# A conformer, gated linear attention and banded attention kernel on one core: VectorE takes part of the lower halves, and the copies of the bias go out in four

## The reference

```python
def conformer_mixer(h, w_in, b_in, w_dw, b_dw, norm_g, norm_b, w_out, b_out):
    u = h @ w_in + b_in
    a, ga, z = jnp.split(u, 3, axis=-1)
    glu = a * jax.nn.sigmoid(ga)
    c = lax.conv_general_dilated(
...
    c = jax.nn.silu(layer_norm(c, norm_g, norm_b))
    return (c * jax.nn.silu(z)) @ w_out + b_out
...
        h = layer_norm(DN_ALPHA * h + y, post_ln_g[i], post_ln_b[i])
...
    bias = rel_bias.astype(jnp.float32)[t5_bucket(rel)]
```

## Time and profile before

| what | value |
|---|---|
| median of 3 runs | 2415.98 us (2415.59 to 2420.63) |
| the profiled execution, its own time | 2417.53 us |
| its span | 2415.8 us |
| PE busy | 2328.9 us, 96% |
| DVE, ACT, POOL busy | 1385.9, 1126.7, 876.8 us |

### The profile page before, as it was taken

How to read it: one execution, slowest core, us unless ns; L and a number is a source line. 1 busy time by engine, 2 the same in 40 slices (tenths; PEclk the granted TensorE clock), 3 DMA queues, 4 the chain that set the end, 5 groups by cost and what they waited for, 6 DMA issues and landing times. The chain is left out here.

```text
span 2415.8 us, 34621 instructions
## 1 busy us (share of the span) xinstructions
PE 2328.9 (96%) x13338; PEld 1215.4 (50%) x13338; DVE 1385.9 (57%) x2328; ACT 1126.7 (47%) x2181; POOL 876.8 (36%) x673
## 2 busy tenths in 40 slices
PE   8999999998997999999999998989899999999998
PEld 4555555543444455555555554444545554444443
DVE  6999999975554234334334334577467777235422
ACT  7766666576653234334334333233246666323311
POOL 3988888877883110100101101344023333000000
PEclk9999999998998999999999999999999999999999
DMA  5011111143333000100000002533100000101222
GB/s 204 27 55 40 39 45 35 49 137 100 115 125 138 28 1 5 53 1 32 18 1 14 1 1 94 100 121 115 62 23 15 19 1 2 40 18 64 103 105 88
DMA packets 52218, 134.67 MB, mean 56 GB/s; under 512 B 5391, under 2 KB 23439, under 8 KB 51032
## 3 DMA queue, kind: packets, MB, share of 16 engines
q1 hardware_dynamic: 52056, 132.46, 16.5%
HBM read 96.65 MB, written 35.80 MB: 55 GB/s over the span
## 5 line engine op out<-in xcount | busy, mean ns | idle before, releaser
L1155 DVE SCALAR_TENSOR_TENSOR cv_tap_sum<-cv_glu,cv_prm,cv_tap_sum 128x1024 f32<-128x1024 f32 x326 | 418.9, 1288 | 11.9 <-ACT cv_tap_sum L657 2.4
L911 POOL TENSOR_TENSOR mixed<-mixed,cv_tap_products 128x1024 f32<-128x1024 f32 x153 | 364.2, 2381 | 77.6 <-ACT cv_tap_products L672 62.1
L100 PE MATMUL cv_proj<-H_hi,cv_w_ga 128*128 128x416 f16 (+1 forms) x640 | 217.2, 339 | 8.1 <-DVE H_lo L1128 8.1
L101 PE MATMUL cv_proj<-H_lo,cv_w_ga 128*128 128x416 f16 (+1 forms) x640 | 217.2, 339 | 0.0
L102 PE MATMUL cv_proj<-H_hi,cv_w_ga 128*128 128x416 f16 (+1 forms) x640 | 217.1, 339 | 0.0
L100 PE MATMUL gm_vr<-gm_wvr_hi,H_hi 128*128 128x512 f16 (+1 forms) x544 | 202.8, 373 | 0.0
L101 PE MATMUL gm_vr<-gm_wvr_lo,H_hi 128*128 128x512 f16 (+1 forms) x544 | 202.8, 373 | 0.0
L102 PE MATMUL gm_vr<-gm_wvr_hi,H_lo 128*128 128x512 f16 (+1 forms) x544 | 202.8, 373 | 0.0
L1823 POOL TENSOR_TENSOR gm_q_inter<-gm_q_rel,gm_block_decays 128x512 f32<-128x512 f32 x16 | 16.8, 1049 | 467.1 <-ACT gm_block_decays L1900 467.1
L672 ACT ACTIVATE cv_tap_products<-cv_glu,cv_prm 128x1024 f32<-128x1024 f32 x138 | 151.8, 1140 | 35.8 <-POOL mixed L911 35.7
L2179 DVE SCALAR_TENSOR_TENSOR gm_v_r<-gm_vr,gm_v_r 128x256 f32<-128x256 f32 x64 | 27.2, 425 | 236.8 <-ACT gm_v_r L1919 236.8
(11 more groups left out here) (449 smaller groups left out, 5783.3 us busy)
## 6 DMA issues: line engine op xcount, KB each, us to landing
cv_w_stage<-conv_w SPq DMA_DIRECT2D x24, 512.0 KB, 4.0
mixed<-gla_w SPq DMA_DIRECT2D x8, 1024.0 KB, 6.9
go_rows<-h_rows SPq DMA_DIRECT2D x16, 512.0 KB, 4.1
h_rows<-go_rows SPq DMA_DIRECT2D x16, 512.0 KB, 2.9
pl_sums_a<-h_rows SPq DMA_DIRECT2D x16, 512.0 KB, 3.5
out<-pl_sums_a SPq DMA_DIRECT2D x16, 512.0 KB, 2.6
cv_tap_products<-gate_z SPq DMA_DIRECT2D x24, 256.0 KB, 3.9
mixed<-xT SPq DMA_DIRECT2D x12, 416.0 KB, 8.7
```

The source lines that it names most:

```text
L100: nc.tensor.matmul(out, w_hi, x_hi, start=first, stop=False)
L101: nc.tensor.matmul(out, w_hi, x_lo, start=False, stop=False)
L911: nc.gpsimd.tensor_tensor(c_unit(U), c_unit(U), prod[:, r % 3, :], ALU.add).then_inc(s_add, 1)
L1155: nc.vector.scalar_tensor_tensor(out=acc_unit(U), in0=window(U, k), scalar=col(U // 2, k), in1=acc_unit(U), op0=ALU.mult, op1=ALU.add).the ...
```

## The change

In the convolution's rows, ACT copies the sums of group 2 in the middle of gating group 1, and those of groups 3 and 4 before it scales the row of that step and not after it. VectorE makes 11 of the lower halves in place of POOL: `LOWS_AT` gives the step, the group and the tiles. The bias of the output is fetched and scaled ahead of the first gating of group 1, and two more gates of that group are loaded ahead of the norm's vectors. The last row is transposed into banks of its own, its scaling comes in two halves, and DVE does the lower half of row 14 ahead of the last row's g and b. In the output layer the bias table is written in four pieces of two heads, in steps 4 to 7 behind the load of the row, where it was one piece in step 2. The k weights are split at the end of step 14 and not at the start of step 15.

```diff
+        LOWS_AT = {3: (2, (5,)), 4: (2, (6, 7)), 7: (3, (4, 5)), 8: (3, (6, 7)), 11: (4, (4, 5)), 12: (4, (6, 7))}
+        DVE_LOWS = [T * KT + k for T, ks in LOWS_AT.values() for k in ks]
...
         pt = [acc[:, HALF + 512 * h:HALF + 512 * h + 512] for h in range(2)]
+        last_pt = [acc[:, 512 * h:512 * h + 512] for h in range(2)]
...
+        def turned(s, h):
...
+        def wait_low(eng, n):
+            by_dve = sum(x < n for x in DVE_LOWS)
+            if by_dve:
+                eng.wait_ge(c_lod, by_dve)
+            eng.wait_ge(c_lo, n - by_dve)
...
@@ -581,18 +596,18 @@
                 load_row(0)
                 for b in range(2):
                     sp.wait_ge(s_szo[b], 16 * KT * NTT // 2)
-                sp.wait_ge(s_add, slot(UNITS - 1, n_products(UNITS - 1)) + 1)
-                for k in range(R):
-                    load_gate(1, k)
                 sp.wait_ge(o_lo, KT)
                 vector(bias_bc, bias_dram, s_bv)
                 load_row(1)
+                sp.wait_ge(s_add, slot(UNITS - 1, n_products(UNITS - 1)) + 1)
+                for k in range(R + 2):
+                    load_gate(1, k)
                 sp.wait_ge(c_m, KT)
                 vector(g_bc, g_dram, s_vec)
                 vector(b_bc, b_dram, s_vec)
                 for s in range(NS + 1):
                     if s == 0:
-                        for k in range(R, KT):
+                        for k in range(R + 2, KT):
...
                 squares(2, range(CG))
-                gated(1, range(2))
                 act.wait_ge(s_bv, 16)
                 nc.scalar.activation(bias_bc, bias_bc, ACT.Copy, scale=1.0 / ALPHA).then_inc(s_bias, 1)
+                gated(1, range(2))
                 squares(2, range(CG, KT))
+                gated(1, range(2, 6))
+                copy_sums(2)
+                gated(1, range(6, KT))
                 for s in range(NS + 2):
-                    gated(*UNITS_AT.get(s, (0, ())))
-                    if (s, 0) in SUMS:
-                        copy_sums(SUMS[s, 0])
+                    if s:
+                        gated(*UNITS_AT.get(s, (0, ())))
...
+                                                 turned(s - 2, h).rearrange("p (k n) -> p k n", k=4)[:, :, 0:n],
+                                                 ACT.Copy).then_inc(s_th, 1)
+                    if (s, 1) in SUMS:
+                        copy_sums(SUMS[s, 1])
...
                         act.wait_ge(s_nm, s + 1)
-                        nc.scalar.activation(tile(s), tile(s), ACT.Identity, scale=sd[0:n, b, 1:2],
...
-                        copy_sums(SUMS[s, 1])
+                        for h in range(2) if s == LAST else (slice(0, 2),):
+                            x = tile(s).rearrange("p (a n) -> p a n", a=2)[:, h]
+                            mm = nc.scalar.activation(x, x, ACT.Identity, scale=sd[0:n, b, 1:2], bias=sd[0:n, b, 2:3])
...
                         gate(T, k)
-                        if i:
+                        if i and T * KT + ks[i - 1] not in DVE_LOWS:
                             low(T, ks[i - 1])
-                    if len(ks):
+                    if len(ks) and T * KT + ks[-1] not in DVE_LOWS:
                         low(T, ks[-1])
...
                                         pattern=[[-1, P]], channel_multiplier=1).then_inc(s_id, 1)
+                add_bias(0)
                 gated(1, range(2))
-                add_bias(0)
...
-                        if s:
+                        if s == LAST:
+                            pe.wait_ge(c_n, len(GROUPS) * KT)
+                        elif s:
...
-                            mm = nc.tensor.transpose(pt[h][:, q * P:q * P + n], tile(s)[:, c:c + P], ident[0:n, 0:n])
+                            mm = nc.tensor.transpose(turned(s, h)[:, q * P:q * P + n], tile(s)[:, c:c + P], ident[0:n, 0:n])
...
-                        pe.wait_ge(c_lo, (T + 1) * KT)
+                        wait_low(pe, (T + 1) * KT)
...
+                def gated_low(T, k):
+                    dve.wait_ge(c_hi, T * KT + k + 1)
+                    nc.vector.tensor_tensor(c_half(T, k, 1), silu_at(T, k), c_half(T, k, 0), ALU.subtract).then_inc(c_lod, 1)
...
-                    if s == LAST:
...
+                                                    turned(s - 2, h).rearrange("p (k n) -> p k n", k=4)[:, :, 0:n],
                                                     H_hi[:, 4 * h:4 * h + 4, at:at + n], ALU.subtract).then_inc(s_tl, 1)
+                    if s in LOWS_AT:
+                        T, ks = LOWS_AT[s]
+                        for k in ks:
+                            gated_low(T, k)
+                    if s == LAST:
+                        for h in range(2):
+                            c = slice(h * 512, h * 512 + 512)
+                            dve.wait_ge(s_vec, 16 * 2)
+                            dve.wait_ge(s_u, NS + h)
+                            nc.vector.tensor_tensor(tile(LAST)[:, c], tile(LAST)[:, c], g_bc[:, c], ALU.mult).then_inc(s_lg, 1)
+                            dve.wait_ge(s_lg, h + 1)
+                            nc.vector.tensor_tensor(tile(LAST)[:, c], tile(LAST)[:, c], b_bc[:, c], ALU.add).then_inc(s_lh, 1)
...
+        COPIES = range(4, 4 + HEADS // 2)
...
                 for s in range(NR):
-                    if s == 2:
-                        sp.wait_ge(s_bs, 1)
-                        rows = bass.AP(copies.tensor, copies.offset, [[(P + 1) * PITCH, HEADS], [PITCH, P + 1], [1, PITCH]])
-                        sp.dma_start(rows, spread_rows(vec, P + 1)).then_inc(s_bo, 16)
                     if s >= 2:
                         store_row(s - 2)
                     if 4 <= s + 1 < NR:
                         load_row(s + 1)
+                    if s in COPIES:
+                        heads = slice(2 * COPIES.index(s), 2 * COPIES.index(s) + 2)
+                        sp.wait_ge(s_bs, 1)
+                        rows = bass.AP(copies.tensor, copies.offset + heads.start * (P + 1) * PITCH,
+                                       [[(P + 1) * PITCH, 2], [PITCH, P + 1], [1, PITCH]])
+                        sp.dma_start(rows, spread_rows(vec[heads, :], P + 1)).then_inc(s_bo, 16)
...
-                    if s == END:
-                        act.wait_ge(ahead.sem, next_loaded)
-                        nc.scalar.activation(wkv[0][:, 0].rearrange("p k n -> p (k n)"), attn_slot(M, 0), ACT.Copy,
-                                             scale=WS).then_inc(s_kh, 1)
...
+                    if s == END - 1:
+                        act.wait_ge(ahead.sem, next_loaded)
+                        nc.scalar.activation(wkv[0][:, 0].rearrange("p k n -> p (k n)"), attn_slot(M, 0), ACT.Copy,
+                                             scale=WS).then_inc(s_kh, 1)
...
-                    if s == END:
-                        dve.wait_ge(s_bo, 16)
-                        dve.wait_ge(s_kh, 1)
...
+                    if s == END - 1:
+                        dve.wait_ge(s_bo, 16 * len(COPIES))
+                        dve.wait_ge(s_kh, 1)
```

More of the change, by code:

```diff
@@ L299, in conv_layer @@
         c_d, c_n, c_sl, c_m = m.sem("c_centred"), m.sem("c_normed"), m.sem("c_silu"), m.sem("c_gated")
-        c_hi, c_lo = m.sem("c_hi"), m.sem("c_lo")
+        c_hi, c_lo, c_lod = m.sem("c_hi"), m.sem("c_lo"), m.sem("c_lo_by_dve")
         c_sz = [m.sem(f"siluz_loaded{k}") for k in range(KT)]
@@ L450, in in_two @@
             return ap.rearrange("p (a n) -> p a n", a=2)
+        def turned(s, h):
+            return (last_pt if s == LAST else pt)[h]
         def n_of(s):
@@ L737, in silu @@
                         if k >= R0:
-                            act.wait_ge(c_lo, n - R0 + 1)
+                            wait_low(act, n - R0 + 1)
                     elif n >= KT + R:
-                        act.wait_ge(c_lo, n - R + 1)
+                        wait_low(act, n - R + 1)
                     else:
@@ L883, in _ @@
                             nc.scalar.activation(H_hi[:, 4 * h:4 * h + 4, at:at + n],
-                                                 pt[h].rearrange("p (k n) -> p k n", k=4)[:, :, 0:n], ACT.Copy).then_inc(s_th, 1)
+                                                 turned(s - 2, h).rearrange("p (k n) -> p k n", k=4)[:, :, 0:n],
+                                                 ACT.Copy).then_inc(s_th, 1)
+                    if (s, 1) in SUMS:
+                        copy_sums(SUMS[s, 1])
                     if s < NS:
@@ L889, in _ @@
                         act.wait_ge(s_nm, s + 1)
-                        nc.scalar.activation(tile(s), tile(s), ACT.Identity, scale=sd[0:n, b, 1:2],
-                                             bias=sd[0:n, b, 2:3]).then_inc(s_u, 1)
-                    if (s, 1) in SUMS:
-                        copy_sums(SUMS[s, 1])
+                        for h in range(2) if s == LAST else (slice(0, 2),):
+                            x = tile(s).rearrange("p (a n) -> p a n", a=2)[:, h]
```

(28 more changed lines are left out.)

## The result

The changed kernel takes **2450.97 us** (median of 4 runs, 2450.25 to 2452.25) where the kernel before took 2415.93 in runs on the same chip: a ratio of 1.0139, interval 1.0127 to 1.0151. It is slower. The forecast was 2448.6 with a range of 2412 to 2464. The profiled span grew from 2415.8 to 2449.7 us, by 33.9, against a forecast of 32.6.

The account below looks back on a forecast made before the run. PE works nearly all of the span, so only its waits can go or new ones come. Convolution +13.5, table pieces +23.5 and k weights -4.4 make +32.6 on 2415.98: 2448.6 us, range 2412 to 2464.

Parts of the forecast that it names:

- A: Convolution, sums of group 2: ACT's copies start sooner, the 7.03 us wait goes, all behind moves by -3.6 us.
- B: Convolution, row 5: waits for DVE's lower halves behind row 4's work, +3.8 us, with the restart +5.4.
- C: Convolution, row 9: waits for DVE's halves like row 5, +12.7 us, with the restart +14.3.
- D: Convolution, row 13: DVE's halves, slowed beside POOL, start it 8.5 us after row 12's end; convolution then at +17.2.
- E: Convolution's end: own banks and split scaling let the last transposes start sooner, -3.7 us; convolution in all +13.5.
- F: Output layer, bias table: each piece takes 21.5 us and delays row loads, +23.5 us at row 11; chance 0.60.
- G: Output layer's end: k weights split a row sooner, so last norms and transposes come 4.4 us sooner.
- Rival H: Output layer: pieces run at their engines' rate, 11 us each, so not slower: 2414.1 us; chance 0.17.
- J: Output layer: each head keeps its rate, 43 us a piece, row 11 another 86 later: about 2535 us; chance 0.10.
- K: Output layer: pieces of about 16 us or on different engines: 2426.7, up to 2436 us; chance 0.13 with L.
- L: Convolution: row 5 doesn't wait for DVE's halves, so it gains 7.3 us: 2427.8 us; counted in K's chance.

Follow-up runs that it names:

- both losses undone: The changed kernel with all lower halves on POOL and the table's pieces of heads four partitions apart: 2393.79 us, ratio 0.9903 to the kernel before.

## Why the prediction was right, point by point

The prediction gave 2448.6 us and a loss from two causes, VectorE's halves behind a row's own work and pieces read from neighbouring partitions. Both are what the experiments found. Shifts are between the traces of before and after; forecast in brackets.

- **A, right.** Row 2 began at 554.54 (554.95), released by POOL. The transposes behind group 2's chain moved from 584.87 to 580.75, by -4.1 (-3.6).
- **B, right.** Row 5 at 612.13 (612.6). Its products took 12.80 us (612.13 to 624.93), so the restart cost 2.4 and not 1.6. PE waited 12.31 and not some 9: it was done with row 4 9.2 us sooner than before (the transposes at 598.78 for 607.94) and not 3.6, since the sums of group 3 came sooner too, a gain that the forecast hadn't. It was lost at row 5, which starts by DVE's time; with all halves on POOL it counts.
- **C, right.** The totals of group 4 at 657.13 (657.3), row 9 at 673.13 (672.5). The wait of 12 us that the prediction's last part names is a slip: its own terms give about 7, and it was 8.08.
- **D, right.** DVE had row 12's second half at 720.05; row 13 began at 728.22, 8.4 after the row's end (8.5). That POOL holds DVE here was read from the earlier trace rows, and the 3.43 for 1.29 shows it.
- **E, right in size**, -4.2 (-3.7): PE's last full row ended 19.7 us later (755.03 before, 774.70 after), the next layer began 15.5 later. **Convolution +15.5 (13.5)**; the 2 us are the restarts, which the forecast priced by the one row of before with a short idle. The transposes behind the last full row (778.54) were still released by `H_lo`, and only those of the last row by DVE's b. The GLA layer gave 1.1 back, not forecast.
- **F, right in mechanism and size**: 21 us a piece (21.5). The estimate from the port figure of the Trainium skill, "SBUF — State Buffer", section "Door 1: The DMA port swizzle (why `[64,N]` ≈ `[32,N]`)", gave 19.1; the rate was 25 GB/s here and not 27.6. Row 9's load was used at 1663.23; the forecast, moved by the 14.4 of the layers ahead, says 1665.6. Row 11 at 1674.69 (1677.1). F cost +21.4 up to the transposes at 1731.93 (23.5). My reason, that two heads share something, is shown by the heads four apart: 25 to 51 GB/s on two engines. The halfway value itself was a choice between the far bounds of 11 and 43, and that it came out so near was luck; it did since two neighbours now share what four shared before. What it lacked: I took the old stall to come of the store queued behind the write alone. On ACT's queue it stayed, with a slow load in the store's place.
- **G, right**: -4.0 at the transposes that it names (1708.67 before, 1740.56 after, row 15 having ended 35.9 later; forecast -4.4). Up to the last transposes it is -5.6, and -5.2 alone: the 1.6 more are TensorE's clock, which before was at a mean of 0.66 from 1708 to 1712 and now was 1.00 in the same place.
- **Not forecast, +3.6** behind the output layer: attention and its last stretch took 3.0 us longer (the last stretch at a lower clock, below), 0.4 lie in the change of layers, and 0.2 behind them.

Sum: 15.5 - 1.1 + 21.4 - 5.6 + 3.6 = 33.8, of the span's 33.9. The terms missed by +2.0, -1.1, -2.1, -1.2 and +3.6; that this leaves 1.2 is luck, too.

Rival H (pieces at their engines' rate) is what happens with heads four apart: 2420.38, where H said 2414.1. Of the 6.3 between them, 1.4 lie in the convolution (the next layer at 786.49, 14.9 later than before), 2.9 in attention (321.1 us for 318.2), and 1.7 in the kernel before itself, which took 2417.64 in those runs. J (each head keeps its rate) is refuted by the window of 25 GB/s for two heads where eight had 49. K (pieces of 16 us, or on different engines): a piece took 21, and in the window from 1604 to 1612 two engines were busy though a further piece had been issued at 1599.38, so pieces didn't run side by side. L is refuted by the waits of B to D.

## What to carry to other kernels

Before work is moved to an engine with idle time, look at what stands ahead of it there in the same step: an engine that is 57% busy can still be the last one that a row waits for, if the helper's work stands behind the row's own. Time it beside what the other engine does then, too: two halves took 1.29 us by themselves and 3.43 beside POOL's scaling. When a transfer from few partitions is slow, look at which partitions it reads before it is cut into pieces; a cut changes how often others wait for it, a stride changes how long it lasts. Where a change has many parts, an experiment that undoes each shows a version that keeps the good ones: here 57 us lay between it and the whole.

## What the runs showed of the hardware

**Neighbouring partitions.** A write from partitions 0 to 7 ran at 49 GB/s on eight engines, two heads side by side at 25 on two, two heads four apart at 51 on two, eight heads four apart at 224 on eight. The 25 for two and the 49 for eight fit groups of four partitions that share 25; distances other than one and four were not run. The Trainium skill, "SBUF — State Buffer", section "Door 1: The DMA port swizzle (why `[64,N]` ≈ `[32,N]`)", has partitions 0 to 3 on one port and gives 27.6 GB/s measured for it; the 25, and the 49 for two ports, agree within 12%.

**The price of a restart.** It doesn't follow from the length of the wait, and no run here shows what it does follow from. Of the kernel with both losses undone, PE at rows 5, 9 and 13, with the transposes that end each, and the clock in the first 4 us of the last two:

```profile
602.45 0.39 PE L100 MATMUL cv_proj<-cv_w_ga,mixed 128*128 128x512 f16 x1 [2.36 <-POOL mixed L960]
...
612.82 1.04 PE L1075 MATMUL cv_tap_sum<-cv_first_sums_ident,cv_glu 128*128 128x128 f32 x8
...
655.03 0.39 PE L100 MATMUL cv_proj<-cv_w_ga,mixed 128*128 128x512 f16 x1 [2.08 <-POOL mixed L960]
...
667.09 1.04 PE L1075 MATMUL cv_tap_sum<-cv_first_sums_ident,cv_glu 128*128 128x128 f32 x8
...
705.20 0.39 PE L100 MATMUL cv_proj<-cv_w_ga,mixed 128*128 128x512 f16 x1 [3.37 <-POOL mixed L960]
...
715.57 1.04 PE L1075 MATMUL cv_tap_sum<-cv_first_sums_ident,cv_glu 128*128 128x128 f32 x8
```

The windows (start and end, us, busy by engine as in the earlier trace rows, clock, DMA share, GB/s):

```profile
655.00:659.00 4.00, 3.97 (x12) 1.57 (x13) 3.09 (x1) 1.87 (x4) 3.92 (x3) 0.62 0.00 0
705.00:709.00 4.00, 3.80 (x18) 1.78 (x19) 1.57 (x4) 2.40 (x3) 3.92 (x3) 1.00 0.00 0
```

After 2.36 and 3.37 us of idle the row took 10.37, as without a wait; the clock behind the 3.37 was 1.00 (2.4 GHz). After 2.08 it took 12.06, with a mean clock of 0.62 in its first 4 us, so mostly at 0.50 (1.2 GHz). The price of a short wait was 0 or 1.7 here, and 2.8 for the 3.88 us with VectorE's halves in three steps; behind the long ones of the changed kernel it was 2.4 to 2.7. Row 5 there, after 12.31 us of idle:

```profile
612.00:616.00 4.00, 3.87 (x10) 1.40 (x11) 4.00 (x8) 1.88 (x3) 1.21 (x1) 0.50 0.01 2
616.00:625.00 9.00, 9.00 (x41) 4.00 (x40) 1.54 (x3) 1.26 (x2) 8.92 (x7) 0.94 0.10 29
```

The first 4 us went at 0.50, and the next 9 not yet all at 1.00.

**The same far behind.** Attention's last stretch, for which no wait was changed, took 30.1 us in the kernel before and 31.7 in the changed one. Their clocks:

```profile
2028.00:2068.00 40.00, 33.84 (x304) 18.10 (x304) 20.65 (x39) 19.02 (x49) 12.33 (x10) 1.00 0.00 1
```

and of the changed kernel:

```profile
2060.00:2102.00 42.00, 35.48 (x306) 19.23 (x304) 20.78 (x40) 19.02 (x49) 12.37 (x10) 0.96 0.00 1
```

It took 30.1 us in four of the ten other kernels as well (all halves on POOL, heads four apart, halves in three steps, the write on ACT's queue) and 31.7 in six, one of the two fastest (both losses undone) among them. Attention ahead of it took 318.2, 319.5 or 321.1 us. So differences of up to 3 us between variants can be this, and nothing that was edited.
